# Input norms over three engines, an early start of the last experts, and offsets added on GpSimd: one change to a two-layer hybrid attention and expert kernel

## The chip, the cores and the metric

The kernel runs on one core of one Trainium2 chip. The metric is the device time of one execution in microseconds. A core has five engines with a queue of instructions each: TensorE (PE in the profile) multiplies matrices into eight banks of PSUM, VectorE (DVE) and ScalarE (ACT) work on elements, GpSimd (POOL) works on elements and issues indirect transfers, SyncE (SP) issues the other transfers. Engines wait for each other by semaphores. "Granted clock" is the share of full TensorE speed that the chip allowed.

## The reference

512 tokens of width 1024 pass through an input norm and two layers. Each layer is three kinds of attention merged by gates, a norm, 32 experts of which each token uses two, and a norm:

```python
h = layer_norm(x, ln_in_g, ln_in_b)
for l in range(DEPTH):                       # DEPTH = 2
    m = hybrid_mixer(h, cos, sin, w_in[l], ...)
    h = layer_norm(DEEPNORM_ALPHA * h + m, ln1_g[l], ln1_b[l])
    f = grouped_moe(h, w_router, b_router, w_gate[l], w_up[l], w_down[l])
    h = layer_norm(DEEPNORM_ALPHA * h + f, ln2_g[l], ln2_b[l])
return h
```

`layer_norm` is `(x - mu) * rsqrt(var + 1e-5) * g + b` over the 1024 columns. An expert is `(silu(x @ w_gate) * (x @ w_up)) @ w_down` with an inner width of 512. The matrices are float32.

## The kernel before

h lies in four tiles of 128 tokens by 1024. Products that need full precision split both sides into a high half (rounded, float32r) and a low half (the rest) and multiply three times (L757 to L759): `hT_hi` and `hT_lo` hold h transposed, `w_hi` and `w_lo` the weights, in units of 128 columns of the weight matrix that pass through two buffers. The first three units of a layer are the index weights ("idx"): 104 columns with the index keys (`index_logits`, bank "ik"), then two units of index queries.

**The norms.** `input_norm` (key ln0) and `returned_norm` (key ln2) run on VectorE. Per tile: statistics in two halves (L1565), their aggregate and the added epsilon (L1572, L1575), the centring `(h - mu) * g` (L1588 from PSUM in two halves, L1593 from SBUF), and `h * rstd + b` (L1596). GpSimd makes rstd from the variance by a power (`inverse_root`, L2127). TensorE then transposes the tile in eight pieces of 128 columns (`transpose_tile`, L742), ScalarE takes the high half from PSUM (L1237) and VectorE the low half (L1552), 512 columns each. After the transposes of tiles 2 and 3 stand two and four idle matmuls of 512 columns (`transpose_h`, L752), whose result nobody reads. `split_first` makes high and low half of the first two idx units, on ScalarE between tiles 1 and 2, on VectorE before the low half of the last tile. The index products of the next layer begin when banks 0 to 3 have been read, that is, when all four tiles are there.

**The expert loop.** Each of the 32 experts has three weight pieces of 2 MB, gate, up and down, 96 in a layer, which SyncE streams into 12 slots in a fixed order; a piece is loaded when its slot's previous piece has been used. TensorE runs over the experts: `gates(e + 1)` (16 pairs of matmuls, L1060 and L1061, and the transposes of the rows of the expert after it, L1050), then the transposed hidden rows (L1067) and `down` (L1078) of expert e. ScalarE copies the result (L1230) and GpSimd scatters it to memory (L2148). For the last expert, 31, gate and up are loaded in four quarters each (L677), down in four quarters too (L682), and TensorE waits for them quarter by quarter. Before the gates of expert 30 TensorE runs five idle matmuls (`idle_products`, L1116), after those of expert 31 three.

**The end of a layer.** SyncE loads the ln2 parameters (L687), then h (L690), waits for the last result and the scattered rows, loads the returned rows `got`, eight loads (L702), and in the first layer the idx weights of the second (L568). TensorE multiplies h by alpha into PSUM (`residual`, L1162) and adds the returned rows with their weights (`returned`, L1172), tile by tile; each tile's two banks "c" then go to `returned_norm`. In the last layer a tile is stored when its norm is done (L712).

An f32 matmul shows as two rows in the trace, a transpose and an f32r matmul as one.

## Time and profile before

| | us |
|---|---|
| median of three runs | 2278.38 |
| lowest and highest | 2276.97, 2281.16 |
| the profiled execution | 2278.19 |
| its span, first to last instruction | 2276.4 |
| TensorE busy | 2056.1 (90%) |
| VectorE busy | 956.1 (42%) |
| ScalarE busy | 674.4 (30%) |
| GpSimd busy | 195.4 (9%) |

The mean granted clock is 0.973. The first layer's expert loop lies between about 665 and 1119 us, the second's between about 1788 and 2241; there the transfers run at some 425 GB/s. In a timeline row the columns are start, duration, engine, line, operation, output and inputs, shapes, and in brackets the idle time before it with what ended it. Rows that follow each other with the same text are merged (x8), and the duration then reaches from the first start to the last end, so that it also holds the drain of the last one. A release is inferred from semaphore events. The chain named in a row can hide an earlier wait, so the start times count more than the names.

### The profile page before, as it was taken

What the parts mean: (1) busy time and instruction counts of PE and PEld (TensorE: products, weight loads), DVE (VectorE), ACT (ScalarE), POOL (GpSimd) and SP (SyncE); (2) the same over time, 40 slices, a digit from 0 to 9 for tenths busy, and PEclk for the clock granted to TensorE, in tenths of its full rate; (3) what the DMA queues carried; (4) which work ended last, traced back from release to release, by engine and by line L of the source; (5) the groups of instructions that cost most, each with busy time, mean ns of one, the idle gap of its engine ahead of it and who ended that gap; (6) DMA issues with size and microseconds to landing.
All of it is one profiled execution on the core that took longest, in us unless ns stands there. A gap on an engine that the chain in (4) does not pass through costs nothing.

```text
span 2276.4 us, 29903 instructions
## 1 busy us (share of the span) xinstructions
PE 2056.1 (90%) x10000; PEld 1226.0 (54%) x10000; DVE 956.1 (42%) x1930; ACT 674.4 (30%) x1390; POOL 195.4 (9%) x244
## 2 busy tenths in 40 slices
PE   6999999999979988788989999999998799887887
PEld 4777876877743333222357678668777333222232
DVE  6865845645651111011178667555456411110113
ACT  4345544544210000000043536546551010000000
POOL 3000001000011111111000000010001111111110
PEclk9999999999989999989999999999999899999999
DMA  6221321323489999999833112113235999999996
GB/s 206 75 75 38 111 75 38 111 75 121 167 336 421 425 424 426 426 426 424 330 132 111 38 61 102 61 38 111 75 130 198 406 424 425 425 425 425 426 422 244
DMA packets 96420, 535.58 MB, mean 235 GB/s; under 512 B 13936, under 2 KB 16880, under 8 KB 73472
## 3 DMA queue, kind: packets, MB, share of 16 engines
q1 hardware_dynamic: 84288, 510.41, 55.6%
q0 software_dynamic: 11968, 23.11, 2.7%
q8 instruction: 88, 1.44, 0.3%
q14 instruction: 76, 0.62, 0.1%
HBM read 527.17 MB, written 23.07 MB: 242 GB/s over the span
## 4 chain that ended last, share of the span: by engine, by line
PE 73%; DVE 9%; issue 6%; DMA 6%; ACT 3%; another core or an unknown queue 2%; POOL 0%; DVEq 0%; SPq 0%; POOLq 0%; ACTq 0%
PE ps L1060 18%; PE ps L757 11%; PE ps L759 11%; PE ps L758 11%; PE ps L1078 9%; DMA scr<-in_w_up 4%; PE ps L856 2%; PE ps L907 2%; PE ps L878 2%; PE ps L1050 1%; DVE scr L2081 1%; DMA scr<-h_rows,scr 1%; ACT scr L1273 1%; PE ps L1162 1%
## 5 line engine op out<-in xcount | busy, mean ns | idle before, releaser
L2061 DVE COPY scr<-ps 128x512 f32<-128x512 f32 x64 | 44.3, 692 | 746.9 <-PE ps L1050 746.9
L757 PE MATMUL ps<-hT_lo,w_hi 128*128 128x512 f32 (+1 forms) x816 | 328.6, 403 | 7.2 <-DVE w_lo L1541 4.8
L759 PE MATMUL ps<-hT_hi,w_hi 128*128 128x512 f32 (+1 forms) x816 | 318.9, 391 | 0.0
L758 PE MATMUL ps<-hT_hi,w_lo 128*128 128x512 f32 (+1 forms) x816 | 317.8, 389 | 0.0
L1061 PE MATMUL ps<-scr 128*64 128x512 f32 x480 | 233.7, 644 | 0.0
L1230 ACT ACTIVATE scr<-ps 128x512 f32<-128x512 f32 (+1 forms) x200 | 103.7, 519 | 327.7 <-PE ps L1078 308.9
L1250 ACT ACTIVATE w_hi<-ring 128x1024 fp32r<-128x1024 f32 x122 | 129.2, 1059 | 224.8 <-PE ps L759 190.8
L1541 DVE TENSOR_TENSOR w_lo<-ring,w_hi 128x1024 fp32r<-128x1024 f32 x122 | 149.2, 1223 | 104.4 <-ACT w_hi L1250 99.8
L1482 ACT ACTIVATE scr<-ps 64x512 f32<-64x512 f32 x64 | 37.7, 589 | 522.2 <-PE ps L1061 522.2
L757 PEld LDWEIGHTS ps<-hT_lo,w_hi 128*128 128x128 f32 (+1 forms) x816 | 153.0, 187 | 42.0 <-DVE w_lo L1541 5.0
L759 PEld LDWEIGHTS ps<-hT_hi,w_hi 128*128 128x128 f32 (+1 forms) x816 | 152.8, 187 | 34.0
L758 PEld LDWEIGHTS ps<-hT_hi,w_lo 128*128 128x128 f32 (+1 forms) x816 | 153.3, 188 | 29.7 <-issue 0.3
L1357 ACT ACTIVATE scr<-ps,small 128x128 f32<-128x128 f32 (+1 forms) x192 | 99.6, 524 | 152.7 <-DVE small L1726 152.1
L1060 PE MATMUL ps<-spare,scr 128*64 128x512 f32 x256 | 121.8, 632 | 22.8 <-DMA scr<-in_w_up 20.9
L1078 PE MATMUL ps<-ring,scr 128*64 128x512 f32 x512 | 116.9, 598 | 23.2 <-DVE scr L2081 23.2
L1726 DVE TENSOR_REDUCE small<-ps 128x2 f32<-128x256 f32 (+1 forms) x96 | 78.7, 822 | 128.5 <-PE ps L867 76.5
L1060 PE MATMUL ps<-scr 128*64 128x512 f32 x224 | 111.7, 657 | 22.9 <-DMA scr<-in_w_up 22.9
L1060 PE MATMUL ps<-ring,scr 128*64 128x512 f32 x256 | 115.8, 606 | 16.9 <-issue 16.9
L2148 POOL DMA_INDIRECT y_halves<-scr x64 | 64.9, 1015 | 753.8 <-ACT scr L1230 651.9
L1078 PE MATMUL ps<-xslot,scr 128*64 128x512 f32 x448 | 102.3, 598 | 20.3 <-DVE scr L2081 20.3
L1061 PE MATMUL ps<-ring,scr 128*64 128x512 f32 x256 | 116.0, 607 | 0.0
L1060 PE MATMUL ps<-h,scr 128*64 128x512 f32 x224 | 103.5, 617 | 10.3 <-DMA wslot<-in_w_up 10.3
(262 smaller groups left out, 3420.2 us busy)
## 6 DMA issues: line engine op xcount, KB each, us to landing
ring<-in_w_down SPq DMA_DIRECT2D x32, 2048.0 KB, 45.7
ring<-in_w_in SPq DMA_DIRECT2D x30, 2048.0 KB, 8.0
scr<-in_w_up SPq DMA_DIRECT2D x28, 2048.0 KB, 46.3
xslot<-in_w_down SPq DMA_DIRECT2D x26, 2048.0 KB, 50.4
spare<-in_w_gate SPq DMA_DIRECT2D x16, 2048.0 KB
ring<-in_w_gate SPq DMA_DIRECT2D x16, 2048.0 KB, 43.6
ring<-in_w_up SPq DMA_DIRECT2D x16, 2048.0 KB, 47.7
wslot<-in_w_up SPq DMA_DIRECT2D x14, 2048.0 KB, 50.8
```

The costliest lines, as they stand in the source:

```text
L757: mm(out, a[0], b[1], start=first, stop=False)
L758: mm(out, a[1], b[0], start=False, stop=False)
L759: return mm(out, a[0], b[0], start=False, stop=last)
L1060: mm(bank[b].t[0:C, :], rows, wg[:, k, :], start=(k == 0), stop=(k == KD - 1))
L1061: ins = mm(bank[b].t[C:2 * C, :], rows, wu[:, k, :], start=(k == 0), stop=(k == KD - 1))
L1078: ins = mm(bank[b].t[half * C:(half + 1) * C, :], hidT[n][:, f, :], w[:, f, half * 512:(half + 1) * 512], start=(f == 0), stop=(f == FE - 1))
L1230: nc.scalar.activation(dst, src, ACT.Copy, scale=scale).then_inc(bank[b].read, 1)
L1250: nc.scalar.activation(unit_part(w_hi, name, q), raw_unit(name, q), ACT.Copy).then_inc(hi_ready.sem, hi_ready.tick((name, q)))
L1357: nc.scalar.activation(pbuf[:, n % 2, j, 0:W], bank[b].t[:, 0:W], ACT.Exp, bias=neg_max[n % 2][:, j:j + 1], accum_out=psum_row[n % 2][:, j ...
L1541: V.tensor_tensor(unit_part(w_lo, name, q), raw_unit(name, q), unit_part(w_hi, name, q).bitcast(F32), ALU.subtract).then_inc(lo_ready.sem, ...
L1726: V.tensor_reduce(neg_max[n % 2], ps[:, b:b + 2, 0:W], AX.X, ALU.max, negate=True).then_inc(max_ready.sem, max_ready.tick((br, n)))
L2148: pool.indirect_dma_start(out=y_halves, out_offset=bass.IndirectOffsetOnAxis(ap=y_now[n] if idx is None else idx, axis=0), in_=ysb[n], in_ ...
```

## The change

1. Input norm and the norm between the layers: VectorE centres, ScalarE scales by rstd (`scale`, a copy with a factor), and the offset b comes into the transposed h by TensorE: each transpose of 128 columns is followed by a product of the offset's one row with a row of ones, added in the same place. h itself gets the offset at the start of each layer, by four additions on VectorE.
2. The index keys are multiplied in two parts, columns 0 to 383 when the first three tiles are there, columns 384 to 511 after the fourth. Each of the first two idx units is waited for by itself. VectorE makes the low half of the second unit after that of the last tile of h (opening), or both before the first statistics (between the layers).
3. The idle matmuls in the transposes: four of 256 columns before tile 3, none after it. Between the layers tile 0 is transposed before the fourth tile of returned rows.
4. Gate and up of expert 30 come in quarters as those of expert 31 do, and the five idle matmuls before them are gone.
5. SyncE: h is loaded before the ln2 parameters, and the idx weights of the next layer right after these, ahead of the wait for the last result. The experts' overflow path (not taken in the trace) uses the ring slots 1 to 3.
6. In the last layer the offset is added after the scaling: tiles 0 to 2 on GpSimd after its last root, tile 3 on VectorE; the stores wait for those.

```diff
@@ SyncE @@
+                    def gate_up_quarters(e, landed):
+                        gate_s, up_s = (slots[expert_slot(e, m)] for m in range(2))
+                        for m in range(2):
+                            used(piece_ahead(piece_no[e, m]))
+                        for q in range(4):
+                            cut = slice(q * UNIT, (q + 1) * UNIT)
+                            for w, s in ((w_gate, gate_s), (w_up, up_s)):
+                                sp.dma_start(s[:, cut], w[one, e:e + 1].rearrange("o q p c -> p (o q c)")[:, cut]
+                                             ).then_inc(landed[q].sem, landed[q].tick("gu", 16))
                     for n in range(XRING, 3 * EPT - 3):
+                        if PIECES[n] == (EPT - 2, 0):
+                            gate_up_quarters(EPT - 2, near_gu)
+                        if PIECES[n][0] == EPT - 2 and PIECES[n][1] < 2:
+                            continue
                         used(piece_ahead(n))
                         expert_piece(n, None)
...
+                    used(H_LAST)
+                    sp.dma_start(h[:, :, :], ...)
                     used(LN_LAST)
                     for src, dst in zip((ln2_g, ln2_b), ln_params["ln2"]):
...
-                    used(H_LAST)
-                    sp.dma_start(h[:, :, :], ...)
+                    used(max(n for n in range(3 * EPT) if SLOT_OF[n] == in_slot["idx"]))
+                    with sp.If(l < DEPTH - 1):
+                        index_weights(slice(DEPTH - 1, DEPTH), "idx next")
                     multiplied(("y", EPT - 1))
...
-                    with sp.If(l < DEPTH - 1):
-                        index_weights(slice(DEPTH - 1, DEPTH), "idx next")
...
-                    sp.wait_ge(h_ready.sem, h_ready.at(("ln2", t), DEPTH - 1))
+                    ready = last_ready if t == NT - 1 else out_ready
+                    sp.wait_ge(ready.sem, ready.at(("out", t)))
@@ TensorE @@
                             ins = nc.tensor.transpose(bank[b].t[:, k * P:(k + 1) * P],
                                                       h[:, t, kd * P:(kd + 1) * P], ident)
+                            if key != "ln1":
+                                ins = mm(bank[b].t[:, k * P:(k + 1) * P], ln_params[key][1][0:1, kd * P:(kd + 1) * P],
+                                         ident[0:1, 0:1].to_broadcast([1, P]), start=False, stop=True,
+                                         skip_group_check=True)
...
-                        for w in range((0, 0, 2, 4)[t]):
+                        for w in range((0, 0, 4, 0)[t]):
...
+                    pe.wait_ge(hT_ready.sem, hT_ready.start(l) - 1)
                     w = unit("idx", 0, l)
...
-                    for k in range(KD):
-                        ins = split_product(bank[b].t[0:KEY_W, :], w(k), hT(k), k == 0, k == KD - 1)
+                    for cut in (slice(0, (NT - 1) * P), tok(NT - 1)):
+                        if cut.start:
+                            pe.wait_ge(hT_ready.sem, hT_ready.start(l))
+                        for k in range(KD):
+                            ins = split_product(bank[b].t[0:KEY_W, cut], w(k), hT(k, cut), k == 0, k == KD - 1)
...
-                        if e == EPT - 3:
-                            idle_products(5, i)
...
-                    for t in range(NT):
+                    for t in range(NT - 1):
                         returned(t, l)
                     with pe.If(l < DEPTH - 1):
-                        transpose_h("ln2", l)
+                        transpose_tile("ln2", 0, l)
+                    returned(NT - 1, l)
+                    with pe.If(l < DEPTH - 1):
+                        transpose_h("ln2", l, 1)
@@ ScalarE @@
+                def scale(key, t, l=0):
+                    if key == "ln2":
+                        for half in range(2):
+                            in_sbuf(c_bank(t, half), ("c", t, half), l)
+                    else:
+                        act.wait_ge(centred.sem, centred.at((key, t), l))
+                    act.wait_ge(rstd_ready.sem, rstd_ready.at((key, t), l))
+                    nc.scalar.activation(h[:, t, :], h[:, t, :], ACT.Copy, scale=rstd[:, t:t + 1]).then_inc(
+                        h_ready.sem, h_ready.tick((key, t)))
...
+                    for t in range(NT + 1):
+                        if t < NT:
+                            scale("ln2", t, l)
+                        if t >= 1:
+                            with act.If(l < DEPTH - 1):
+                                take_hT("ln2", l, (t - 1,))
@@ VectorE @@
+                    with dve.If(l < DEPTH - 1):
+                        split_first("next", l)
-                    for t in range(NT + 3):
+                    for t in range(NT + 2):
...
                             moments_done("ln2", t, l)
-                        if 1 <= t < NT + 1:
-                            normalise("ln2", t - 1, l)
-                        if t > 2:
+                            normalise("ln2", t, l)
+                        if t > 1:
...
+                    dve.wait_ge(h_ready.sem, h_ready.start(l))
+                    for t in range(NT):
+                        V.tensor_tensor(h[:, t, :], h[:, t, :], ln_params["ln0"][1], ALU.add).then_inc(
+                            h_full.sem, h_full.tick("h"))
@@ GpSimd @@
+                book.scope = "post"
+                for t in range(NT - 1):
+                    pool.wait_ge(h_ready.sem, h_ready.at(("ln2", t), DEPTH - 1))
+                    alone(pool)
+                    G.tensor_tensor(h[:, t, :], h[:, t, :], ln_params["ln2"][1], ALU.add).then_inc(
+                        out_ready.sem, out_ready.tick(("out", t)))
```

In the opening VectorE's queue reads so, from the centring of the first tile on, before:

```order
L1593 SCALAR_TENSOR_TENSOR h<-h,moments,scr 128x1024
L1596 SCALAR_TENSOR_TENSOR h<-h,rstd,scr 128x1024
L1593 SCALAR_TENSOR_TENSOR h<-h,moments,scr 128x1024
L1596 SCALAR_TENSOR_TENSOR h<-h,rstd,scr 128x1024
L1552 TENSOR_TENSOR hT_lo<-ps,hT_hi 128x4x128 x2
```

and after, to the start of the first layer:

```order
L1649 SCALAR_TENSOR_TENSOR h<-h,moments,scr 128x1024 x2
L1602 TENSOR_TENSOR hT_lo<-ps,hT_hi 128x4x128 x2
L1649 SCALAR_TENSOR_TENSOR h<-h,moments,scr 128x1024
L1602 TENSOR_TENSOR hT_lo<-ps,hT_hi 128x4x128 x2
L1649 SCALAR_TENSOR_TENSOR h<-h,moments,scr 128x1024
L1602 TENSOR_TENSOR hT_lo<-ps,hT_hi 128x4x128 x2
L1616 TENSOR_TENSOR w_lo<-ring,w_hi 128x832
L1602 TENSOR_TENSOR hT_lo<-ps,hT_hi 128x4x128 x2
L1616 TENSOR_TENSOR w_lo<-ring,w_hi 128x1024
L2066 UNCONDITIONAL_BRANCH
L2066 ISA
L2071 TENSOR_TENSOR h<-h,scr 128x1024 x4
```

The second pass over h is gone from each tile, and four additions stand behind the low halves, in the layer's body.

TensorE's queue at the end of the expert loop, with what each row waits for, before (down of expert 28, the idle matmuls, the first gate and up product of expert 30):

```order
L725 REGISTER_ALU [waits land0]
L733 REGISTER_ALU [waits bank6_read]
L1078 MATMUL ps<-ring,scr 64x512 [waits bank3_read]
L1078 MATMUL ps<-ring,scr 64x512 x7
L725 REGISTER_ALU
L1116 MATMUL ps<-scr,cf 128x512 [waits bank6_read]
L1116 MATMUL ps<-scr,cf 128x512 x4
L1095 REGISTER_ALU [waits bank0_read]
L1060 MATMUL ps<-ring,scr 64x512 [waits bank2_read,land3,land1]
L1061 MATMUL ps<-ring,scr 64x512
```

and after, to the second quarter:

```order
L742 REGISTER_ALU [waits land0]
L750 REGISTER_ALU [waits bank6_read]
L1105 MATMUL ps<-ring,scr 64x512 [waits bank3_read]
L1105 MATMUL ps<-ring,scr 64x512 x7
L1085 ISA [waits bank2_read,bank0_read]
L1087 MATMUL ps<-ring,scr 64x512 [waits near_gu0]
L1088 MATMUL ps<-ring,scr 64x512
L1087 MATMUL ps<-ring,scr 64x512
L1088 MATMUL ps<-ring,scr 64x512
L1087 MATMUL ps<-ring,scr 64x512 [waits near_gu1]
```

The five idle matmuls are gone, and the wait for both whole pieces (land3, land1) is now one for a quarter, before the first pair and after each second one.

GpSimd's queue at the end of the program, after (before it ends with the branch of L2190, which is L2259 here):

```order
L2196 TENSOR_TENSOR rstd<-small,cf 128x1
L2259 REGISTER_ALU
L2259 COMPARE_AND_BRANCH
L2342 TENSOR_TENSOR h<-h,scr 128x1024 x3
L521 UNCONDITIONAL_BRANCH
```

The three additions stand behind the fourth root and the loop's branch.

## Rows read from the trace of the kernel before

**Rows 1.** Busy time in stretches of the second expert loop, late and later; GB/s last

```profile
core 0: us, PE busy (x) PEld busy (x) DVE busy (x) ACT busy (x) POOL busy (x), PEclk, DMA share, GB/s
2190.00:2200.00 10.00, 8.47 (x42) 3.38 (x40) 0.57 (x1) 1.19 (x2) 2.04 (x2) 1.00 1.01 427
...
2220.00:2225.00 5.00, 4.48 (x26) 1.53 (x24) 0.42 (x1) 0.60 (x1) 1.00 (x1) 1.00 1.03 413
```

**Rows 2.** Timeline of SyncE's issues: start, duration, what is loaded

```profile
1128.82 4.87 SPq L568 DMA_DIRECT2D ring<-in_w_in  x2
...
2155.73 4.11 SPq L638 DMA_DIRECT2D ring<-in_w_up  x1
...
2206.52 4.28 SPq L677 DMA_DIRECT2D spare<-in_w_up  x1
...
2220.37 0.93 SPq L690 DMA_DIRECT2D h<-h_rows  x1
```

**Rows 3.** DMA issues from 2150 us on: KB each, median us to landing

```profile
ring<-in_w_up SPq DMA_DIRECT2D x1, 2048.0 KB, 50.8
...
spare<-in_w_up SPq DMA_DIRECT2D x4, 512.0 KB, 20.7
...
h<-h_rows SPq DMA_DIRECT2D x1, 2048.0 KB, 19.6
```

**Rows 4.** Timeline of TensorE at the end of the second expert loop

```profile
2204.94 4.56 PE L1116 MATMUL ps<-scr,cf 128*128 128x512 f32 x10 [0.78 <-ACT scr L1230]
...
2209.43 0.64 PE L1060 MATMUL ps<-ring,scr 128*64 128x512 f32 x1
...
2232.27 0.59 PE L1060 MATMUL ps<-xslot,scr 128*64 128x512 f32 x1
```

**Rows 5.** Timeline of TensorE after both expert loops: residual, returned rows, index products

```profile
1121.22 8.80 PE L1162 MATMUL ps<-h,norm_g 128*128 128x512 f32 x16 [2.41 <-issue]
...
1129.86 13.90 PE L1172 MATMUL ps<-scr 128*128 128x512 f32 x32
...
1160.15 0.48 PE L757 MATMUL ps<-hT_lo,w_hi 128*104 128x512 f32 x1 [1.12 <-DVE hT_lo L1552]
...
2242.88 7.10 PE L1162 MATMUL ps<-h,norm_g 128*128 128x512 f32 x16 [2.24 <-issue]
...
2249.82 14.11 PE L1172 MATMUL ps<-scr 128*128 128x512 f32 x32
```

**Rows 6.** Timeline of VectorE in the last norm

```profile
2263.04 1.40 DVE L1588 SCALAR_TENSOR_TENSOR h<-ps,moments,scr 128x512 f32<-128x512 f32 x2
...
2265.84 1.29 DVE L1565 BATCH_NORM_STATS2 stats<-ps 128x6 f32<-128x512 f32 x2
...
2267.72 1.40 DVE L1588 SCALAR_TENSOR_TENSOR h<-ps,moments,scr 128x512 f32<-128x512 f32 x2
...
2272.11 1.28 DVE L1596 SCALAR_TENSOR_TENSOR h<-h,rstd,scr 128x1024 f32<-128x1024 f32 x1 [0.19 <-DVE h L1588]
```

**Rows 7.** Timeline of the opening and the first products

```profile
17.58 1.94 PE L742 MATMUL ps<-cf,h 128*128 128x128 f32 x8 [17.58 <-DVE h L1596]
...
22.90 1.83 ACT L1259 ACTIVATE w_hi<-ring 128x832 fp32r<-128x832 f32 x2
...
33.89 0.80 PE L757 MATMUL ps<-hT_lo,w_hi 128*104 128x512 f32 x1
...
39.81 0.39 PE L757 MATMUL ps<-hT_lo,w_hi 128*128 128x512 f32 x1
...
41.11 1.23 DVE L1541 TENSOR_TENSOR w_lo<-ring,w_hi 128x1024 fp32r<-128x1024 f32 x1 [8.31 <-ACT w_hi L1250]
```

**Rows 8.** Timeline of TensorE in the first attention: narrow products at full clock

```profile
144.96 0.49 PE L856 MATMUL ps<-scr 64*128 64x128 f32 x4
145.39 0.23 PE L862 MATMUL ps<-scr,cb 72*128 72x128 bf16 x1
```

**Rows 9.** Timeline of GpSimd in the opening

```profile
11.48 0.71 POOL L2178 TENSOR_TENSOR scr<-scr 128x256 f32<-128x256 f32 x1
...
17.88 1.38 POOL L2178 TENSOR_TENSOR scr<-scr 128x256 f32<-128x256 f32 x1
...
23.52 1.82 POOL L2183 TENSOR_SCALAR scr<-scr 128x256 f32<-128x256 f32 x1 [0.20 <-POOL scr L2182]
```

More of the change, by code:

```diff
@@ L328, in trunk @@
         hT_hi_ready = signal("hT_hi_ready")
+        hT_ready = signal("hT_ready")
+        centred = signal("centred")
+        h_full = signal("h_full")
+        out_ready = signal("out_ready")
+        last_ready = signal("last_ready")
         dve_seq = signal("dve_seq")
@@ L373, in trunk @@
         last_gu = [signal(f"last_gu{q}") for q in range(4)]
+        near_gu = [signal(f"near_gu{q}") for q in range(4)]
         last_down = [signal(f"last_down{q}") for q in range(4)]
@@ L670, in _ @@
                     last = slice(EPT - 1, EPT)
-                    gate_s, up_s, down_s = (slots[expert_slot(EPT - 1, m)] for m in range(3))
-                    used(piece_ahead(3 * EPT - 3))
-                    used(piece_ahead(3 * EPT - 2))
-                    for q in range(4):
-                        cut = slice(q * UNIT, (q + 1) * UNIT)
-                        for w, s in ((w_gate, gate_s), (w_up, up_s)):
-                            sp.dma_start(s[:, cut], w[one, last].rearrange("o q p c -> p (o q c)")[:, cut]).then_inc(
-                                last_gu[q].sem, last_gu[q].tick("gu", 16))
+                    down_s = slots[expert_slot(EPT - 1, 2)]
+                    gate_up_quarters(EPT - 1, last_gu)
                     used(piece_ahead(3 * EPT - 1))
@@ L1051, in turn_rows, with gate_up @@
                     return ins
-                def gate_up(n, slots, b, last_of=None):
+                def gate_up(n, slots, b, last_of=None, landed=last_gu):
                     wg, wu = cols(slots[0]), cols(slots[1])
@@ L1188, in _ @@
                     book.scope = "layer"
-                    for b in range(4):
-                        pe.wait_ge(bank[b].read, bank[b].full.now(l))
                     index_logits(l)
@@ L1553, in take_hT, with alone_inc, split_first @@
                                         hT_hi[:, dst[0], dst[1]].bitcast(F32), ALU.subtract).then_inc(bank[b].read, 1)
-                def split_first(when, l=0):
-                    for q in range(2):
+                    dve.wait_ge(bank[b].read, bank[b].full.at((key, t, 1), l))
+                    dve.wait_ge(bank[b - 1].read, bank[b - 1].full.at((key, t, 0), l))
+                    alone_inc(hT_ready, (key, t))
+                def alone_inc(sig, key):
+                    dve.sem_inc(sig.sem, sig.tick(key))
+                def split_first(when, l=0, parts=range(2)):
+                    for q in parts:
                         dve.wait_ge(hi_ready.sem, hi_ready.at((when, q), l))
```

69 lines of the change are left out of this document (42 added, 27 removed).

## The prediction

> **What bounds the kernel now.** I read the timeline first, because the change touches only a few short places: the opening, the end of the expert loop in each of the two layers, the norm between the layers, and the last norm. In the expert loop the transfers are the limit: the DMA share stands at 1.0 and the rate at 427 GB/s [rows 1], so a faster engine gains nothing there as long as weights are late. At its very end this turns. The up weights of expert 30 are issued at 2155.73 and land 50.8 us later, at 2206.5 [rows 2, 3]. TensorE is through with the products before them at 2204.2 (2204.94 less the 0.78 of idle time), but then runs ten rows of idle products, 4.56 us, and starts on expert 30 at 2209.43 [rows 4], 2.9 us after the weights. From there on it is TensorE, not DMA, that sets the end. Between the layers VectorE is the chain: TensorE starts the index products at 1160.15, after waiting for the last low half of h [rows 5]. In the last layer VectorE is the chain alone: the returned rows are summed by 2263.93 (2249.82 + 14.11) [rows 5], and tiles that follow each other every 4.68 us (2263.04 to 2267.72) carry it to 2273.39 [rows 6]. In the opening the same chain runs behind transposes at half clock [rows 7].
>
> **The end of the expert loop, twice.** The change removes the five idle matmuls (ten rows) and lets the gate and up weights of expert 30 land in quarters, in turn gate, up, gate, up. Their stream ends at 2206.5 as before, so the quarters land near 2199, 2201.5, 2204 and 2206.5 (4 MB at 427 GB/s is 9.8 us). TensorE can start at 2204.3 and asks for the last quarter after three quarters of 6.9 us, at 2209.5. It does not wait. So it is 5.1 us earlier. What is late next is expert 31: its first product stood at about 2225.8 and its last pair at 2232.27 [rows 4], so the last quarter was asked for at 2231.0, and 5.1 us earlier at 2225.9. That quarter is issued at 2206.52 and lands some 20.7 us later, 2227.2 as a median of four [rows 2, 3]; a stream of eight quarters from 2216.5 gives 2226.7. Quarters also move at 413 instead of 427 GB/s [rows 1], which for 4 MB more is 0.35 us. So 0.6 us of the 5.1 go back into a wait: **4.5 us per layer**, bounds 2.5 and 5.1. The last down quarters follow 5 us later and are then just in time.
>
> h is loaded next. It lands at 2240.0 (2220.37 + 19.6) [rows 2, 3], and TensorE multiplied it from 2242.88. With 4.5 us less it would be wanted at 2238.4, but the change puts it ahead of the two 0.5 MB parameter loads, which is 2.4 us earlier, 2237.6. It stays hidden. In the first layer the 1.4 MB of index weights now stand ahead of the loads of the returned rows. Before, they were issued last, at 1128.82, for 4.87 us [rows 2]. I allow 5 us for their transfer (3.4 us at 413 GB/s and the rest for the 32-byte pieces). They follow the parameters from about 1117 to 1122; the first returned rows are issued at 1119.6 and needed when the residual products end, 1125.3 with the 8.80 us of [rows 5]. They land there, with nothing to spare; up to 1.5 us can be lost.
>
> **Between the layers.** I count from the start of the returned products, R = 1129.86. Before, the index weights' first unit was multiplied at R + 30.3 and took 5.9 us (33.89 to 39.81, the same products in the opening) [rows 5, 7]: R + 36.2. Now the chain is TensorE's. Three tiles of returned rows take 3 x 3.47 = 10.4 us (13.90 over four) [rows 5]. A tile's transposes now have eight offset products of one row each between them. A pair of such f32 products, 128 columns wide, takes 0.43 us (144.96 to 145.39) [rows 8], so one takes 0.21, and a transpose 0.11 at full clock and 0.22 at half (1.94 for eight) [rows 7]. That makes 2.6 us per tile at full clock, 5.2 at half. Tile 0 at 13.0, the fourth returned tile at 16.5, tiles 1 and 2 at 21.7, four idle products half as wide as before (0.9) at 22.6, tile 3 at 25.2. The other engines keep up: VectorE has lost the 1.28 us pass per tile [rows 6] but still has statistics, centring and the low half, and has centred tile 3 at about R + 19.3; ScalarE scales it in 1.1 us (its 832- and 1024-wide copies together take 1.83) [rows 7], before 22.6; the low halves of tiles 0 to 2 are there at 23.2. The split of the index weights, which stood before the last low half, now lies in VectorE's wait for the first returned tile. The index products start at R + 25.2, with 384 columns: 24 x 0.17 = 4.1 us; then 24 more with 128 columns. The trace has no such f32r product. The nearest rows bound it: the 512-wide f32r product takes 0.24 (5.9 over 24 and the gap) [rows 7], so from a quarter of that, 0.06, to all of it; a 128-column transpose with f32 weights takes 0.11. I take 0.11, for the weights are of the same kind: 2.6 us. End at R + 31.9, **4.3 us** earlier, bounds 1.2 and 5.5; I count 4.0, for one more wait between engines.
>
> "TensorE: Matmul & The Clock Gate" of the Trainium skill (Back-to-back issue gap) gives about 81 ns for a stream of 128-column products with their weight loads. It would make the second cut 1.9 us and each layer start 0.7 us better; no row here shows it for f32r.
>
> VectorE's four new additions of the offset to h at the start of each layer (4 x 1.28 = 5.1 us) lie in its idle time, 8.31 us before 41.11 [rows 7]. If that cover were gone they would cost at most their 5.1 us; the low half of the third unit is needed 3 us later than it is made, so I count 0.
>
> **The opening.** The first scaled tile comes at 17.5 as before (centring on VectorE, 1.28, then ScalarE, 1.1). Tile 0 takes TensorE to 22.7 at half clock. Then low half, centring, scaling and transposes pass from engine to engine, tile 2 at 29.1, tile 3 at 33.5, so the index products start at 33.8 against 33.89 [rows 7], and the two cuts take 6.7 instead of 5.9 us. **A loss of 0.8 us**, bounds a gain of 1 (narrow products at 0.06) and a loss of 4 (at 0.23, and 0.4 late).
>
> **The last norm.** Rows are summed at 2263.93; statistics and centring end by 2266.9 (1.88 from the second statistics to the centring, 1.40 for it, less the half already done) [rows 6]. ScalarE scales until 2268.0, VectorE adds until 2269.4. But GpSimd adds to tiles 0 to 2 only after its fourth root, which follows the same statistics: from about 2266.3. Its cost is the disputed one: an addition of 256 columns took 0.71 us alone and 1.38 beside VectorE [rows 9]. Four times that is 2.8 and 5.5; with a fixed part in each, 2.6. Three are 7.8, and 0.5 for VectorE beside the first: 2274.6. Before, the last tile was ready at 2273.39 (2272.11 + 1.28) [rows 6] and the span ended 3.0 later, at 2276.4. Now one more store is issued behind that of tile 2, 0.4: the end would be 2278.0, **a loss of 1.6 us**, bounds a gain of 0.4 (2.1 per addition, nothing lost to VectorE) and a loss of 10 (5.5 per addition).
>
> The "GPSIMD Engine Reference" of the Trainium skill (Elementwise, side-by-side cycle accounting) gives 4497 ns for such an addition of 2048 columns, twice VectorE's, and advises against it. Half of that is 2.25 us, and by it the end would be an estimated 1.1 us better than in my sum. The rule speaks against this part of the change; the rows agree on the direction.
>
> **The sum.** 4.5 + 4.0 + 4.5 - 0.8 - 1.6 = 10.6 us. The profiled execution took 2278.2 with a span of 2276.4, the median of the runs is 2278.4, so the two agree and 2267.8 stands for the median.
>
> **Rivals.** (A) The narrow second cut costs as much as a wide product, 0.23 for each of 24, twice: 2.9 us more each, 2273.6. The trace has no row against it. (B) DMA sets the end of the expert loop after all, because quarters move slower [rows 1] or the waits for both slots open a gap in the stream: 2.0 instead of 4.5 us per layer, 2272.8. Against it: the queue holds 50 us of work [rows 3]. (C) The offset products and the relay between three engines eat the shared norm's gain: 1 instead of 4 us, 2270.8. Against it: VectorE has less to do per tile [rows 6], for it: TensorE has 1.7 us more (2.6 instead of 0.9). (D) Slower: GpSimd stays at the rate of its slowest contended rows. An addition of 7.3 us (1.82 for a 256-column operation beside VectorE [rows 9], times four) makes 14.1 us more, 2281.9. It decides from 6.1 us per addition (2.6 + 10.6 / 3). Against it: VectorE is idle after the first of the three. (E) Additions near 2 us, narrow products at 0.06 and a full clock where the residual products ran partly at half (8.80 against 7.10) [rows 5]: 2262.
>
> **How the numbers follow.** Forecast 0.63, A 0.09, B 0.09, C 0.08, D 0.05, E 0.06. What these runs can tell from no change is 0.2%, 4.6 us; A lies on that edge. So faster 0.88, within 0.07, slower 0.05. The range takes in all but D and the tails: 2262 to 2274.
>
> **What would show it.** No idle products ahead of expert 30 and its products some 5 us earlier; a wait for weights in expert 31 under 1 us; index products in two cuts of about 4 and 2.6 us, the first from 25 us after the returned products; GpSimd's three additions last in the chain, each near 2.6 us. The prediction is wrong if expert 31 waits over 2 us, if the 128-wide products take over 0.2 us, or if an addition takes over 4 us.

## The result, and the profile after

| | before | after |
|---|---|---|
| median of the runs, us | 2277.7 | 2320.9 |
| span of the profiled execution, us | 2276.4 | 2317.8 |

The changed kernel is slower: the ratio is 1.0185 with a 95% interval of 1.0172 to 1.0199, some 43 us where the prediction had a gain of 10.6. (Experiments that ran on another chip have a median of before of 2280.5 or 2280.6 there. Their ratios are against it; a difference in us between kernels from different chips is good to some 3 us only.)

The two spans differ by 41.4 us. The timelines, laid side by side at the places of the prediction, put it here:

| place | shift of after against before | since the last place |
|---|---|---|
| first product of the unit after the index keys, layer 0 | 63.50 - 39.81 | +23.7 |
| residual products at the end of layer 0 | 1140.97 - 1121.22 | -3.9 |
| first product of the unit after the index keys, layer 1 | 1203.56 - 1165.77 | +18.0 |
| residual products at the end of layer 1 | 2280.94 - 2242.88 | +0.3 |
| first returned product, layer 1 | 2289.58 - 2249.82 | +1.7 |
| end | 2317.8 - 2276.4 | +1.6 |

For the place in layer 1 the prediction had worked out R + 36.2, which is 1166.1. The row of the kernel before stands 0.3 earlier, at R + 35.9:

```profile
1165.77 0.39 PE L757 MATMUL ps<-hT_lo,w_hi 128*128 128x512 f32 x1
```

Two places lose nearly all of it, and both are the shared norm. The 1.7 us further down are the residual products: they take 8.8 us here and took 7.1, at a granted clock of 0.83 (2280 to 2290) instead of 1.00 (2242 to 2250 before). This is TensorE in the opening of the changed kernel (start, duration, engine, line, tiles, idle time); L759 is a transpose, L763 an offset product, L774 the idle products, L779 to L781 the index products:

```profile
18.99 0.47 PE L759 MATMUL ps<-cf,h 128*128 128x128 f32 x1
...
19.39 0.79 PE L763 MATMUL ps<-cf,scr 1*128 1x128 f32 x2
...
20.12 0.47 PE L759 MATMUL ps<-cf,h 128*128 128x128 f32 x1
...
44.90 3.78 PE L774 MATMUL ps<-cf 128*128 128x256 f32 x8
...
50.08 0.33 PE L759 MATMUL ps<-cf,h 128*128 128x128 f32 x1
...
50.33 0.48 PE L763 MATMUL ps<-cf,scr 1*128 1x128 f32 x2
...
50.75 0.33 PE L759 MATMUL ps<-cf,h 128*128 128x128 f32 x1
...
55.13 0.65 PE L779 MATMUL ps<-hT_lo,w_hi 128*104 128x384 f32 x1
55.58 0.52 PE L780 MATMUL ps<-hT_hi,w_lo 128*104 128x384 f32 x1
```

Durations overlap, so read the distance between starts. In these opening rows read the speed from that distance too: up to 44 us the granted-clock column says 1.00 for both kernels, though the rows run at the slower speed. A transpose and its offset product together take 1.13 us at the slower clock (18.99 to 20.12) and 0.67 at the faster (50.08 to 50.75). A tile has eight such pairs: 9.0 and 5.4 us, where the prediction had 5.2 and 2.6. The first index product starts at 55.13 instead of 33.89 [rows 7]. Nothing waits for another engine in between: TensorE itself is the chain.

Between the layers the same happens, and the granted clock falls with it (per stretch: us; busy us and count of PE, weight loads, DVE, ACT, POOL; granted clock; DMA share; GB/s):

```profile
1170.00:1180.00 10.00, 10.00 (x37) 5.98 (x36) 3.76 (x7) 2.23 (x3) 0.55 (x1) 0.78 0.15 54
1180.00:1190.00 10.00, 10.00 (x28) 6.57 (x28) 1.38 (x2) 1.19 (x2) 0.00 (x0) 0.54 0.07 15
1190.00:1200.00 10.00, 10.00 (x37) 7.51 (x36) 1.52 (x3) 2.48 (x3) 0.00 (x0) 0.66 0.02 6
```

The last norm went nearly as predicted (GpSimd, VectorE, SyncE):

```profile
2305.56 7.92 POOL L2342 TENSOR_TENSOR h<-h,scr 128x1024 f32<-128x1024 f32 x3
...
2307.48 1.51 DVE L2181 TENSOR_TENSOR h<-h,scr 128x1024 f32<-128x1024 f32 x1 [1.29 <-ACT h L1293]
2308.00 6.37 SPq L729 DMA_DIRECT2D out<-h  x4
```

Three additions take 7.92 us, 2.64 each (predicted 2.6), last in the chain.

### The profile page after: what moved, and what is told of

The parts are those of the page before. It is cut to its first block, busy times and chain, and to the rows that moved or that the text cites. A ratio compares the mean times of both kernels' runs of the same rounds, so it can differ in the third digit from the quotient of the medians.

```text
span 2317.8 us, 30323 instructions
## 1 busy us (share of the span) xinstructions
PE 2100.2 (91%) x10140; PEld 1256.3 (54%) x10148; DVE 952.9 (41%) x1927; ACT 688.3 (30%) x1402; POOL 200.8 (9%) x247
## 3 DMA queue, kind: packets, MB, share of 16 engines
HBM read 527.17 MB, written 23.07 MB: 237 GB/s over the span
## 4 chain that ended last, share of the span: by engine, by line
PE 70%; DMA 9%; DVE 7%; issue 5%; ACT 2%; another core or an unknown queue 2%; SPq 2%; POOL 1%; DVEq 0%; POOLq 0%; ACTq 0%
PE ps L1087 16%; PE ps L779 11%; PE ps L781 11%; PE ps L780 11%; PE ps L1105 7%; DMA ring<-in_w_up 4%; PE ps L883 2%; DMA scr<-in_w_up 2%; PE ps L934 2%; PE ps L905 2%; DMA h<-h_rows 2%; PE ps L763 2%; PE ps L1203 1%; PE ps L1077 1%
## 5 line engine op out<-in xcount | busy, mean ns | idle before, releaser
L779 PE MATMUL ps<-hT_lo,w_hi 128*128 128x512 f32 (+2 forms) x832 | 334.7, 402 | 6.1 <-DVE w_lo L1591 4.9
L781 PE MATMUL ps<-hT_hi,w_hi 128*128 128x512 f32 (+2 forms) x832 | 324.7, 390 | 0.0
L780 PE MATMUL ps<-hT_hi,w_lo 128*128 128x512 f32 (+2 forms) x832 | 324.0, 389 | 0.0
L1088 PE MATMUL ps<-scr 128*64 128x512 f32 x480 | 218.4, 609 | 0.0
L779 PEld LDWEIGHTS ps<-hT_lo,w_hi 128*128 128x128 f32 (+1 forms) x832 | 157.7, 190 | 40.4 <-DVE w_lo L1591 5.0
L781 PEld LDWEIGHTS ps<-hT_hi,w_hi 128*128 128x128 f32 (+1 forms) x832 | 157.4, 189 | 33.5
L780 PEld LDWEIGHTS ps<-hT_hi,w_lo 128*128 128x128 f32 (+1 forms) x832 | 158.0, 190 | 29.0
L1087 PE MATMUL ps<-ring,scr 128*64 128x512 f32 x256 | 124.5, 643 | 22.4 <-DMA ring<-in_w_up 22.4
L1105 PE MATMUL ps<-ring,scr 128*64 128x512 f32 x512 | 118.5, 605 | 24.4 <-DVE scr L2145 22.5
L1087 PE MATMUL ps<-spare,scr 128*64 128x512 f32 x256 | 116.1, 607 | 21.2 <-DMA scr<-in_w_up 19.5
L1087 PE MATMUL ps<-h,scr 128*64 128x512 f32 x224 | 108.9, 643 | 19.2 <-DMA wslot<-in_w_up 19.2
L1088 PE MATMUL ps<-ring,scr 128*64 128x512 f32 x256 | 124.5, 643 | 0.0
L1087 PE MATMUL ps<-scr 128*64 128x512 f32 x224 | 102.0, 610 | 14.3 <-DMA scr<-in_w_up 14.3
```

Of the source, the lines that this page charges most:

```text
L779: mm(out, a[0], b[1], start=first, stop=False)
L780: mm(out, a[1], b[0], start=False, stop=False)
L781: return mm(out, a[0], b[0], start=False, stop=last)
L1087: mm(bank[b].t[0:C, :], rows, wg[:, k, :], start=(k == 0), stop=(k == KD - 1))
L1088: ins = mm(bank[b].t[C:2 * C, :], rows, wu[:, k, :], start=(k == 0), stop=(k == KD - 1))
L1105: ins = mm(bank[b].t[half * C:(half + 1) * C, :], hidT[n][:, f, :], w[:, f, half * 512:(half + 1) * 512], start=(f == 0), stop=(f == FE - 1))
```

## Experiments on the offset products

The first theory: changing between transpose mode and an ordinary product empties TensorE each time. Its edits, all in `transpose_tile`:

**Without the offset products.**

```
-                            if key != "ln1":
-                                ins = mm(bank[b].t[:, k * P:(k + 1) * P], ln_params[key][1][0:1, ...],
-                                         ident[0:1, 0:1].to_broadcast([1, P]), start=False, ...)
```

> The changed kernel without the 64 offset products between the transposes (so the transposed h lacks the offset; the output is computed from it). Theory (alternating a transpose with an ordinary f32 product is what costs): a tile's transposes fall from 9.0 us (half clock) and 5.4 us (full) to about 1.9 and 0.9 us, the first index product starts at about 34 us instead of 55, and with both norms the kernel takes about 2321 - 22 - 16 = 2283 us. Rival (the clock, not the products: only four idle products half as wide instead of six wide ones): the transposes are quick but the index products still run at half clock for some 10 us, and the kernel stays above 2290.

The index products start at 30.38 us, 24.8 earlier than in the changed kernel and 3.5 earlier than before:

```profile
30.38 0.42 PE L774 MATMUL ps<-hT_lo,w_hi 128*104 128x384 f32 x1 [1.15 <-DVE w_lo L1611]
```

So the offset products are the whole loss of the opening, the clock included, and the rival of the idle products falls. The whole took 2317.9 us. With other values of h the router sends tokens elsewhere, and the expert part does other work: this kernel reads 533.72 MB where the changed one reads 527.17, and 6.5 MB is about one expert's three pieces more. So only the opening can be compared, which is a flaw of the experiment.

**Grouped by four, and skewed by one.**

```
+                        for k in range(4):     # grouped: four transposes first
+                            transpose k
+                        for k in range(4):
+                            offset product k
```

> The same work as the changed kernel, but the four transposes of a bank come first and its four offset products after them. Theory (each change between transpose and product drains TensorE): two changes per bank instead of eight, a tile takes about 3 us at full clock and 5.5 at half instead of 5.4 and 9.0; the opening is some 12 us shorter and the kernel some 20 us faster, about 2300 us. Rival (an offset product is dear by itself, a stationary operand of one row or a moving one read with step 0): nothing changes, 2321 us.

> The same work, alternating as in the changed kernel, but each offset product stands one transpose later, so that it never adds to the 128 columns that the instruction before it wrote. Theory (alternation drains TensorE): as slow as the changed kernel, 2321 us, within 3. Rival (the product waits for the transpose that has just written the same place in PSUM): a tile falls to about 3 us and the kernel to about 2300 us.

These two have the same flaw: h comes out other than in the changed kernel, both read 540.27 MB, and the totals (2389.6 and 2407.0 us) say nothing. The start of the opening can be read. Grouped, two banks:

```profile
16.95 1.09 PE L759 MATMUL ps<-cf,h 128*128 128x128 f32 x4 [16.95 <-ACT h L1294]
17.96 2.07 PE L763 MATMUL ps<-cf,scr 1*128 1x128 f32 x8
19.97 1.11 PE L759 MATMUL ps<-cf,h 128*128 128x128 f32 x4
21.01 2.07 PE L763 MATMUL ps<-cf,scr 1*128 1x128 f32 x8
```

A bank takes 3.04 us instead of 4.5 at the slower clock. The skewed one starts its banks at 16.79 and 20.78, 4.0 us. The expectation for the skewed order was a time as long as the changed kernel's; but it has six changes per bank instead of eight. So the number of changes matters. Adding to columns that the last instruction did not write saves no more than those two changes. That speaks for the theory. But every change here is two changes at once: of the kind, and of the rows, 128 to one.

**Transposes as ordinary products.**

```
-                            ins = nc.tensor.transpose(bank..., h[:, t, kd * P:(kd + 1) * P], ident)
+                                mm(bank..., h[:, t, kd * P:(kd + 1) * P], ident, start=True, stop=False)
```

> The transposes of h in the two shared norms are ordinary f32 products against the identity (four passes, 0.21 us at full clock as any f32 product of 128 columns, against 0.11 for a transpose), with the offset products behind each as in the changed kernel. Theory (alternation between the two kinds is the cost): no alternation is left, a pair takes 0.43 us at full clock, a tile 3.4 instead of 5.4 us, and the clock is at its full level since all is ordinary work; about 2300 us or under. Rival (the offset product is dear by itself): a pair takes 0.67 - 0.11 + 0.21 = 0.77 us, the kernel is slower than the changed one, about 2325 us.

2343.4 us, 1.027 [1.025, 1.029] of before, slower even than the changed kernel. Between the layers, at full clock:

```profile
1207.83 0.48 PE L765 MATMUL ps<-cf,scr 1*128 1x128 f32 x2
1208.24 0.49 PE L763 MATMUL ps<-cf,h 128*128 128x128 f32 x2
1208.66 0.48 PE L765 MATMUL ps<-cf,scr 1*128 1x128 f32 x2
```

0.42 us per product, where 0.21 had been expected, though no change of kind is left. The pair takes 0.83 us, which is longer than the 0.67 with transposes. The first theory falls, and so does the expected 2300 us. Left are two: a product over one row next to one over 128, or any f32 product this narrow.

**The same offsets over 128 rows.** The parameters stand on all 128 partitions, so the identity's first column picks the same values:

```
-    ln_params[key][1][0:1, cols], ident[0:1, 0:1].to_broadcast([1, P])
+    ln_params[key][1][:, cols],   ident[:, 0:1].to_broadcast([P, P])
```

> The changed kernel with the same offsets added by products over 128 rows instead of one (stationary: the offset as it stands on all 128 partitions; moving: the first column of the identity, repeated), alternating with the transposes as before; the computation is the same. Theory (what is left of the cost comes from changing between a product over one row and one over 128 rows, as in the run of ordinary products, where a pair took 0.83 us instead of 0.43): the pair falls from 0.67 us at full clock towards 0.40 (0.25 for the product), from 1.12 to about 0.8 at half, a tile from 5.4 and 9.0 to some 3.3 and 6.3 us, the kernel to about 2305. Rival (changing between transpose and product is the cost, or the product of 128 columns is dear with any number of rows): nothing changes, 2321 within 3.

2276.9 us, 0.9979 [0.9967, 0.9991]: one edit of two operands takes back some 44 us, where 2305 us in all had been expected. At the slower and at the faster clock:

```profile
17.92 0.42 PE L759 MATMUL ps<-cf,h 128*128 128x128 f32 x1
18.14 0.63 PE L763 MATMUL ps<-cf,scr 128*128 128x128 f32 x2
18.56 0.42 PE L759 MATMUL ps<-cf,h 128*128 128x128 f32 x1
...
34.20 0.42 PE L779 MATMUL ps<-hT_lo,w_hi 128*104 128x384 f32 x1 [0.20 <-DVE w_lo L1616]
...
1138.76 0.39 PE L763 MATMUL ps<-cf,scr 128*128 128x128 f32 x2
...
1139.09 0.38 PE L763 MATMUL ps<-cf,scr 128*128 128x128 f32 x2
```

The pair takes 0.64 and 0.33 us: transpose 0.11 and product 0.22 at full clock, the prices of the prediction, with kinds alternating as before.

> Transposes of h in the shared norms as ordinary f32 products and the offset products over 128 rows: no change of kind and no change of rows is left. Theory (change of rows is what costs): 0.21 us per product at full clock, 0.43 per pair against 0.83 in the run with one-row offsets, a tile 3.4 us; the kernel at about 2343 - 8 x (6.6 to 11.6 - 3.4 to 6.8) = 2308, and lower where the denser work brings the clock back. Rival (a 128-column f32 product takes 0.41 us whatever stands before it): 2343 within 3.

2284.3 us, 1.0019 [1.0009, 1.0029], some 58 less than with one row (2308 had been expected); at full clock a product every 0.22 us:

```profile
1140.01 0.39 PE L765 MATMUL ps<-cf,scr 128*128 128x128 f32 x2
1140.24 0.39 PE L763 MATMUL ps<-cf,h 128*128 128x128 f32 x2
1140.46 0.39 PE L765 MATMUL ps<-cf,scr 128*128 128x128 f32 x2
```

**64 and 96 rows.** The same operands, cut to `[0:64]` and `[0:96]`.

> The changed kernel with its offset products over 64 rows instead of one (both operands are the same on those rows as in the 128-row run; the computation is the same). Theory (what costs is the change between products that fill all 128 rows and products that fill few): undecided where 'few' begins; if 64 rows are few, the pair takes 0.67 us at full and 1.12 at half clock as with one row, and the kernel stays at about 2321; if they are not, 0.33 and 0.64 us and about 2277, as with 128 rows. Rival (it is the single row, or operands on one partition, that is dear): 0.33 us, 2277.

> The same with 96 rows. Theory (a product over more than 64 rows takes the whole array like one over 128): 0.33 us per pair, 2277 us. Rival (every number of rows but the transposes' 128 costs a change): 0.67 us per pair, 2321 us.

2319.2 us (1.0156 [1.0135, 1.0177]) and 2277.5 us (0.9985 [0.9972, 0.9998]). 64 rows, slower clock; then 96 rows, faster clock:

```profile
17.11 0.79 PE L763 MATMUL ps<-cf,scr 64*128 64x128 f32 x2
17.83 0.47 PE L759 MATMUL ps<-cf,h 128*128 128x128 f32 x1
18.23 0.79 PE L763 MATMUL ps<-cf,scr 64*128 64x128 f32 x2
18.95 0.47 PE L759 MATMUL ps<-cf,h 128*128 128x128 f32 x1
```

```profile
1145.33 0.27 PE L759 MATMUL ps<-cf,h 128*128 128x128 f32 x1
1145.44 0.39 PE L763 MATMUL ps<-cf,scr 96*128 96x128 f32 x2
1145.66 0.27 PE L759 MATMUL ps<-cf,h 128*128 128x128 f32 x1
```

64 rows cost what one row costs (1.12 us per pair), 96 what 128 cost (0.33). So what is dear is a change between a product over 1 or 64 rows and one over 128, while 96 next to 128 costs nothing; no other row counts were tried here. The price of a change from the pairs, two changes each: (0.67 - 0.33) / 2 = **0.17 us at full clock**, (1.12 - 0.64) / 2 = **0.24 at the slower one**. It fits the runs from which it was not taken. Grouped: four pairs of 0.64 and two changes make 3.0 us (3.04 seen), and at full clock four of 0.33 and two of 0.17 make 1.66 (1.62 to 1.68 seen). Skewed: 2.55 and six changes make 4.0 (4.0 seen). Ordinary products alternating: 0.45 + 0.34 = 0.79 (0.83 seen, so a change is nearer 0.2 there).

The traces also show something that goes with the price. A matmul is preceded by the load of its weights (PEld). With 1 row (and with 64) the load of a transpose begins only with the transpose itself; with 128 rows (and with 96) it begins 0.11 us ahead, under the product before. First the changed kernel, then the one with 128 rows:

```profile
1171.09 0.14 PEld L759 LDWEIGHTS ps<-cf,h 128*128 128x128 f32 x1
1171.09 0.33 PE L759 MATMUL ps<-cf,h 128*128 128x128 f32 x1
```

```profile
1145.98 0.14 PEld L759 LDWEIGHTS ps<-cf,h 128*128 128x128 f32 x1
1146.09 0.27 PE L759 MATMUL ps<-cf,h 128*128 128x128 f32 x1
```

So the change of shape takes away this overlap. Whether that is the whole price is not shown.

## Experiments on the other parts

**The end of the expert loop alone**, in the kernel before: quarters for expert 30, no five idle products.

```
+                        if PIECES[n] == (EPT - 2, 0):
+                            gate_up_quarters(EPT - 2, near_gu)
-                        if e == EPT - 3:
-                            idle_products(5, i)
```

> The kernel before with one part of the change alone: the gate and up weights of expert 30 in quarters and no idle products ahead of them. The prediction's theory: 4.5 us per layer, about 2269 us. Rival (the eight small transfers shorten what the issue queue holds, the down weights of expert 29 land late and TensorE waits for them as it does in the changed kernel, 1.9 us and a down block of 5.3 instead of 3.65): 1 to 2 us per layer, 2274 to 2277 us.

2277.2 us, 0.999 [0.998, 0.9999]: 3.4 us between the medians, not 9. In layer 0 its returned products start 4.2 us earlier than before (1125.67 against 1129.86), near the predicted 4.5. Its last down block there is even 5.3 us earlier, but 1.3 of that goes back in a wait for h, so the agreement is partly luck. In layer 1 its last down block is 2.4 us earlier and the residual products 1.1 (2241.76 against 2242.88):

```profile
2226.20 0.64 PE L1075 MATMUL ps<-xslot,scr 128*64 128x512 f32 x1 [0.53 <-DMA spare<-in_w_up]
...
2228.95 0.64 PE L1075 MATMUL ps<-xslot,scr 128*64 128x512 f32 x1 [0.81 <-DMA spare<-in_w_up]
...
2241.76 3.67 PE L1181 MATMUL ps<-h,norm_g 128*128 128x512 f32 x8 [3.55 <-DMA h<-h_rows]
```

Expert 31 waits twice for its up quarters, and h, which this kernel still loads behind the parameters, is late. The transfers set this end again.

**Additions between the roots.** A version that needs no offset product: the opening norm as before, and after a returned tile VectorE centres, ScalarE scales, GpSimd adds to tiles 0 to 2, VectorE to tile 3.

```
                     for t in range(NT):
                         inverse_root("ln2", t, l)
+                        if t > 0:
+                            pool.wait_ge(centred.sem, centred.at(("ln2", t - 1), l))
+                            G.tensor_tensor(h[:, t - 1, :], h[:, t - 1, :], ln_params["ln2"][1], ALU.add)
```

> A version without the offset products: the opening norm on VectorE as before the change, the norm between the layers and the last one with VectorE centring, ScalarE scaling, GpSimd adding the offset to tiles 0 to 2, each between its roots (root of tile t + 1, then the addition to tile t), VectorE adding to tile 3; the index product in two cuts, the tail as in the changed kernel. The computation is the same. If the offset products were the whole loss: the opening as before or 0.5 us better, the index products between the layers start about 24 us after the returned products instead of 30 (before) and 45 (changed), some 5 us earlier than before, the last tile ready about 5.7 us after the last returned row instead of 9.5, some 2.5 us better than before; with 0 to 4 us per layer of the tail: 2262 to 2270 us. Rival (GpSimd slows to 4 us or more per addition while VectorE works beside it, so that its roots come late): 2272 to 2280 us.

2273.1 us, 0.9965 [0.9954, 0.9976]. An addition takes 2.35 us with VectorE at work beside it, so GpSimd's roots are not late, and in the last norm the tile is ready 5.8 us after the last returned row (2270.61 against 2264.84), as worked out. Between the layers it misses: the index products start 31.6 us after the returned ones, later than the 30.3 of before. The low half of tile 0 stood ahead of the statistics of tile 3 on VectorE and waited for ScalarE.

> The version with GpSimd's additions between its roots, with one more change: between the layers VectorE takes the statistics of all four tiles before it makes the first low half (before, the low half of tile 0 stood ahead of the statistics of tile 3 and waited for ScalarE, so that tile 3 was 3.5 us late). Theory: the index products start about 25 us after the returned ones instead of 31.6, 6 us earlier; if all of it reaches the end 2267 us, if the clock takes back what TensorE gains in the attention behind it as in the other runs, 2270 to 2273 (no change).

2270.1 us, **0.9947 [0.9933, 0.9961]**, the fastest kernel of this study, 10.5 us under before and some 50 under the changed one. The index products start 3.4 us earlier than in the version before it, 28.0 us after the returned ones where 25 had been expected. First they, then the last additions:

```profile
1155.16 0.74 PE L775 MATMUL ps<-hT_lo,w_hi 128*104 128x384 f32 x1
```

```profile
2264.25 2.35 POOL L2320 TENSOR_TENSOR h<-h,scr 128x1024 f32<-128x1024 f32 x1
...
2266.71 1.23 DVE L1683 TENSOR_TENSOR h<-h,scr 128x1024 f32<-128x1024 f32 x1 [1.83 <-POOL h L2320]
```

The four idle products behind tile 3 (1152.13 to 1155) now stand ahead of the index products; that was not taken further.

> The same version with the end of the expert loop as it was before the change: whole gate and up weights of expert 30 and five idle products. Theory (the tail is worth some 2 us in all, as its run alone showed): 2 us more than the version with it. The prediction's 4.5 us per layer: 9 us more. Rival (the tail is worth nothing once the stream of weights sets the end): the same time within 1 us.

2274.7 us, 0.9974 [0.9964, 0.9985]: on top of the new norm the tail is worth 4.6 us, about half of the 9 predicted for both layers, and more than the 2 expected here. Every run of this kernel (2273.05 and up) is above every run of the one with the tail (2272.81 and less), so the difference is there.

## Why the prediction was wrong, step by step

**The offset product.** The step that failed is "a pair of such f32 products, 128 columns wide, takes 0.43 us (144.96 to 145.39) [rows 8], so one takes 0.21". The 0.21 was right for a product over the whole array. The row was of 64-row products following one another, and nothing in it shows what stands between a product over 64 rows and one over 128. The sum priced the product and left out two changes of shape for each, 128 in all, at 0.17 to 0.24 us each. So a tile's transposes took 5.4 and 9.0 us instead of 2.6 and 5.2. By these prices the changes make 14.9 us in the opening (27 pairs at the slower clock, 0.49 each, and 5 at the faster, 0.34) and 12.5 between the layers (11 and 21). What is left of the 23.7 and 18.0 us, some 8 and 6 when set against the run with 128 rows, goes with the clock: the same pairs, idle products and index products also ran longer at the slower clock. The clock was not changed by itself, so this share is inferred. In the opening the transposes with one row run at the slower speed until about 48 us, and again from 53 to 59, over the last of them and the index products; with 128 rows a transpose is down to 0.27 by 23.45 and stays there. Between the layers TensorE did nothing but such pairs from 1170.47 to 1184.97. In that time a pair goes from 0.67 to 1.13 us (at 1175.9), and the granted clock is 0.50, the 1.2 GHz level, in 1180 to 1185. It is still 0.50 in the idle products behind them, 0.88 in 1188.5 to 1193, and 0.50 again in 1193 to 1199. With 128 rows it reads 1.00 from 1130 to 1170. The bounds of this term, 1.2 and 5.5 us, bounded the width of the index product and not the cost of the offset product, which had one row behind it and was treated as known. Rival C, which named the offset products, allowed them 3 us.

**Between the layers, without that.** The 128-row run shows the other steps at 0.5 us gained instead of 4.0: the unit after the index keys starts at R + 35.4 (1163.25 against 1127.83) instead of R + 35.9. The second cut costs 0.09 us per product (predicted 0.11; Rival A, 0.23, falls). The 81 ns of the Trainium skill's "TensorE: Matmul & The Clock Gate" (Back-to-back issue gap) is the nearer figure. Two things were mis-sized. The four idle products of 256 columns took 1.7 us (1150.11 to 1151.83) and not 0.9; in the kernel before, four of 512 columns took 3.0 in the opening (30.85 to 33.89), so its trace could have given the size. And the first index product, to start when tile 3 was transposed (R + 25.2, seen R + 26.8), started at R + 29.0, 0.6 us after VectorE's fourth signal (1156.2):

```profile
1156.80 0.42 PE L779 MATMUL ps<-hT_lo,w_hi 128*104 128x384 f32 x1 [2.13 <-DVEq L1610]
```

The third signal, for which its first cut waits in the code, had come at 1151.7. Why it started only after the fourth is open, but the fourth signal is not a likely cause. In the opening of the same run the first index product starts at 34.2, before the fourth low half. Its weight load stands behind 2.3 us of idle time that the profile puts down to no wait, and ScalarE has the same at that moment:

```profile
1156.79 0.17 PEld L779 LDWEIGHTS ps<-hT_lo,w_hi 128*104 128x104 f32 x1 [2.31 <-issue]
...
1157.50 1.28 ACT L1281 ACT_TABLE_LOAD   x1 [2.20 <-issue]
```

The runs with 96 rows and with ordinary products have it too (2.2 and 1.9 us). Between the layers all engines go from one turn of the layer loop into the next here, in the opening they do not; that fits, but no run isolates it.

**The end of the expert loop.** Layer 0: 4.5 predicted, 4.2 seen in the tail run, 3.9 in the changed kernel: right in size, with the wait for h as a part that was not foreseen. Layer 1: 4.5 predicted; in the tail run 2.4 until h was waited for, which is Rival B's size (2.0). The term mis-sized is expert 31's wait for its quarters: 0.6 us predicted, 0.53 + 0.81 of idle time seen, and with the slower products around it 1.7 to 1.8 us of the lead lost (4.2 us at its start, 2.4 at its last down block); the lead at the start of expert 30 had been 4.1 and not 5.1. In the changed kernel nothing was left of it: down 29, issued behind eight small transfers that each hold SyncE for 2 to 5 us, was late:

```profile
2229.23 6.16 SPq L645 DMA_DIRECT2D ring<-in_w_down  x1
```

```profile
2254.33 5.26 PE L1105 MATMUL ps<-ring,scr 128*64 128x512 f32 x16 [1.92 <-DMA ring<-in_w_down]
```

Its down block waits 1.92 us and then takes 5.26 instead of 3.65. The argument "the queue holds 50 us of work" [rows 3] counted pieces of 2 MB; with quarters in it the landing times fell to 34 us and, for this piece, 24.9. That the quarters made this piece late is not shown: the tail run has the same eight quarters and a landing time of 22.6 us, and no such wait; the 128-row run waits 1.00 us there, and the one with 96 rows and the two with the additions between the roots not at all. Expert 31's two waits for its up quarters, on the other hand, recur in these four runs (0.35 to 0.71 and 0.63 to 1.02 us), though not in the one with ordinary products over 128 rows.

**The opening.** With 128 rows the loss is 0.8 us (the next unit at about 40.65 against 39.81), as predicted. **The last norm.** Predicted loss 1.6 us; from the first returned product to the end 28.2 us against 26.6: 1.6. GpSimd's 2.6 us per addition was right, and Rival D (7.3) falls. That the sum came out to the tenth is partly luck: the additions ended 0.9 us earlier than worked out, and the end came 4.3 us behind them instead of 3.4. The Trainium skill's "GPSIMD Engine Reference" (Elementwise, side-by-side cycle accounting), whose figure halved gave 2.25 us, is close to the 2.35 seen in the version with the additions between the roots. Its advice against GpSimd agrees with the loss where the additions stand last; where they lie between the roots they delay nothing, though no run has them on VectorE there for comparison.

**What became of gained time.** In the tail run the lead of 4.2 us at the first index product of layer 1 is gone before the experts start: a gate product of expert 0 stands at 1786.52 against 1786.50. It goes in single steps of 0.5 to 1.3 us, at places where the granted clock drops for about 3 us, as here:

```profile
1217.00:1219.00 2.00, 2.00 (x6) 1.59 (x5) 1.73 (x4) 0.00 (x0) 0.00 (x0) 0.50 0.00 0
```

Before, the same stretch reads 1.00. That is one execution of each; whether an earlier start brings such drops on, or whether they fall where they will, these runs don't settle. The medians (3.4 and 4.6 us for the tail) say that of the leads in the profiles some part reaches the end.

## What to carry to other kernels

On TensorE, price the changes between instructions along with the instructions: a product over 1 or 64 rows among products over 128 costs little itself and 0.17 to 0.24 us each time the shape changes, and the clock was lower too where the stream was thinned out in this way. If the operand stands on all partitions anyway, as a broadcast parameter does, multiply over 128 rows with a one-hot vector; here that was some 44 us. When a price is read from a row, compare its rows, columns and neighbours with those of the new place. And before moving work to a helper engine, look for gaps in its own chain, since the change lost 1.6 us with the additions behind the last root, while between the roots they delayed nothing.

## What the runs showed of the hardware

- A change between f32 products over 1 or 64 rows and transposes or products over 128 rows takes 0.17 us at full and 0.24 at the slower clock, as the mean of both directions (0.2 at full clock where both products are ordinary ones); between 96 and 128 rows there is none. With it the weight load of the transpose no longer begins 0.11 us ahead. Alternating transposes with ordinary products of the same rows costs nothing (0.11 + 0.22 us at full clock).
- An f32 product of 128 columns over 96 or 128 rows takes 0.22 us at full clock, an f32r one 0.09, a 384-wide f32r one 0.17.
- A GpSimd addition of 128x1024 f32 takes 2.35 us beside a busy VectorE, and 2.64 each for three in a row.
- The grouped and the skewed order gave outputs that differ from the alternating order's, with the same error in both (0.41 relative). Why was not tested by itself; whoever regroups such products should compare the values.
